# A two-layer hybrid decoder on one core: the indexer moved beside the value projection, and two modulation chunks moved to layer 0

## What is computed

```python
mod = c_act @ ada_w[i] + ada_b[i]                    # 6 x 2048 columns per layer
proj = h @ in_w                                      # q, k, v, qi, wi, ki
qi = apply_rope(qi.reshape(B, L, 16, 64)); ki = apply_rope(ki)      # 16 query heads, one key
wi = wi * 16 ** -0.5
s_idx = einsum('bqhd,bsd->bqhs', qi, ki) * 64 ** -0.5
score = einsum('bqh,bqhs->bqs', wi, relu(s_idx))     # one score for each query and key
score = where(causal, score, -inf)
_, sel = top_k(score, 64)                            # 64 of 256 keys for each query
p = softmax(q @ k[sel].T * 128 ** -0.5)              # 16 heads of 128, only on chosen keys
out = (p @ v[sel]) @ out_w
```

## Time and profile before

| | |
|---|---|
| median of 3 runs | 2574.96 us |
| profiled execution, its own time | 2569.49 us |
| its span, first to last instruction | 2567.7 us |
| TensorE busy | 2434.0 us, 95% |
| VectorE busy | 1811.4 us, 71% |
| ScalarE busy | 1042.8 us, 41% |
| mean granted TensorE clock | 0.974 of 2.4 GHz |
| bytes by DMA | 627.35 MB, mean 244 GB/s |

### The profile page before, as it was taken

One profiled execution on the slowest core, in us unless ns is written; L12 is line 12 of the kernel. 1 busy time (PEld: TensorE's weight loads), 2 busy tenths in 40 slices (PEclk: granted clock), 3 DMA queues, 4 the chain that ended last, 5 costly groups with the idle time before them and its releaser, 6 DMA issues.

```text
span 2567.7 us, 33013 instructions
## 1 busy us (share of the span) xinstructions
PE 2434.0 (95%) x12615; PEld 1942.5 (76%) x12615; DVE 1811.4 (71%) x2796; ACT 1042.8 (41%) x1217; POOL 35.3 (1%) x67
## 2 busy tenths in 40 slices
PE   5898789999999999999999999869999999999998
PEld 2475357878888888888878888748888888888886
DVE  6446988867777767777678877787777755455457
ACT  1353024364443434344453444454644344443442
POOL 0000000000000000000000000000000000000000
PEclk9999899999999999999999999789999999999999
DMA  9856988868888887888658888306588766656664
GB/s 339 325 185 254 375 296 288 280 189 281 300 279 301 293 284 266 279 285 280 196 159 283 278 294 278 126 17 231 170 311 284 251 196 194 188 191 192 193 216 146
DMA packets 310172, 627.35 MB, mean 244 GB/s; under 512 B 30240, under 2 KB 30656, under 8 KB 309760
## 3 DMA queue, kind: packets, MB, share of 16 engines
q1 hardware_dynamic: 305728, 611.35, 70.8%
q0 software_dynamic: 4288, 13.90, 1.8%
HBM read 623.05 MB, written 2.10 MB: 243 GB/s over the span
## 4 chain that ended last, share of the span: by engine, by line
PE 83%; DMA 6%; DVE 5%; issue 2%; ACT 1%; SPq 1%; DVEq 0%; ACTq 0%
PE psB L1842 38%; PE psA L1842 38%; DMA col_raw<-in_ada_w 4%; PE psT L1533 1%; PE psM L1576 1%; PE psM L1563 1%; DVE w_lo L950 1%; DMA w_raw<-in_dsa_in_w 1%; DMA w_raw<-in_s_in_w 1%; PE psT L1722 1%; DMA w_raw<-in_s_glu_w 1%; DVE score L1373 1%; PE psM L1548 0%; ACT w_hi L670 0%; PE psM L1545 0%
## 5 line engine op out<-in xcount | busy, mean ns | idle before, releaser
L950 DVE TENSOR_TENSOR w_lo<-w_raw,w_hi 128x1024 fp32r<-128x1024 f32 x748 | 912.5, 1224 | 619.8 <-ACT w_hi L670 615.9
L670 ACT ACTIVATE w_hi<-w_raw 128x1024 fp32r<-128x1024 f32 x748 | 791.9, 1060 | 1170.0 <-PE psB L1842 479.5
L1842 PE MATMUL psA<-w_hi,hT_hi 128*128 128x512 f32 (+1 forms) x1168 | 457.6, 392 | 9.9 <-issue 3.2
L1842 PE MATMUL psB<-w_hi,hT_hi 128*128 128x512 f32 x1152 | 455.8, 396 | 2.9 <-DVE w_lo L950 2.8
L1842 PE MATMUL psA<-w_hi,hT_lo 128*128 128x512 f32 (+1 forms) x1168 | 454.0, 389 | 0.0
L1842 PE MATMUL psA<-w_lo,hT_hi 128*128 128x512 f32 (+1 forms) x1168 | 453.7, 388 | 0.0
L1842 PE MATMUL psB<-w_hi,hT_lo 128*128 128x512 f32 x1152 | 448.8, 390 | 0.0
L1842 PE MATMUL psB<-w_lo,hT_hi 128*128 128x512 f32 x1152 | 448.5, 389 | 0.0
L967 DVE SCALAR_TENSOR_TENSOR ada_acc<-ada_raw,csil,ada_acc 128x512 f32<-128x512 f32 x420 | 314.0, 748 | 15.3 <-DVE ada_acc L967 0.9
L1842 PEld LDWEIGHTS psA<-w_hi,hT_hi 128*128 128x128 f32 x1168 | 221.5, 190 | 57.1 <-issue 8.7
L1842 PEld LDWEIGHTS psB<-w_hi,hT_hi 128*128 128x128 f32 x1152 | 216.3, 188 | 53.3 <-DVE w_lo L950 6.0
(11 more groups left out here) (344 smaller groups left out, 2107.5 us busy)
## 6 DMA issues: line engine op xcount, KB each, us to landing
w_raw<-in_ffn_w_in SPq DMA_DIRECT2D x352, 512.0 KB, 4.5
ada_raw<-in_ada_w SPq DMA_DIRECT2D x448, 256.0 KB, 5.0
w_raw<-in_ffn_w_out SPq DMA_DIRECT2D x176, 512.0 KB, 4.6
col_raw<-in_ada_w SPq DMA_DIRECT2D x160, 512.0 KB, 6.8
w_raw<-in_dsa_in_w SPq DMA_DIRECT2D x112, 512.0 KB, 4.9
w_raw<-in_s_glu_w SPq DMA_DIRECT2D x64, 512.0 KB, 5.5
w_raw<-in_s_in_w SPq DMA_DIRECT2D x32, 512.0 KB, 3.7
w_raw<-in_dsa_out_w SPq DMA_DIRECT2D x32, 512.0 KB, 5.2
```

The lines of the kernel that those rows point to most:

```text
L670: nc.scalar.activation(high(u), w_raw[:, u % RING], ACT.Copy).then_inc(w_hi_ready, 1)
L950: V.tensor_tensor(low(u), w_raw[:, u % RING], high(u).bitcast(F32), ALU.subtract).then_inc(w_lo_ready, 1)
L1842: ins = MM(PS[s][:, t, 0:r.width], a_[:, kt, tok], b_[:, kk, 0:r.width], start=kt == 0 and m == 0, stop=k == r.units - 1 and kk == UK - 1 ...
```

## The change

**The indexer.** The runs of layer 1 are now `rope`, `idx`, `ki`, `v`, `z`. In `ki` the weights are the stationary operand (80 columns) and the activations of all 256 tokens move, so a unit is six matmuls of 256 columns (`key_products`) in place of twelve of 80; ScalarE and VectorE copy and split only the 80 columns. The result lies transposed in psM and is turned back in `v` (`turn_keys`), roped (`rope_keys`), turned again. The 32 score products, the relus, the weighted sums, the mask, the top-k rounds and `selb` are spread over the 32 units of `v`. The buffers moved out of `hT_hi`, which `v` still reads. `attention()` starts with the logits.

**The chunks.** `v` has no chunks any more. ff1 has five (8 to 12) and ff2 four (15 to 18), with a new spread: the pieces lie evenly over all steps of the run but the last six, 80 in 58 steps and 64 in 42. The numbers of the chunks behind them move by one or two. `ada_acc` has two buffers. In these two runs SP has the pieces of a step ahead of the step's weights.

```diff
-                runs += [Run("rope", 4, dsa_in_w[0], (0, NB), layer=1, ada=[(1, 4, 17)], before="ln"),
-                         Run("v", 2, dsa_in_w[0], (2 * D, 2 * D + NB), layer=1, ada=[(0, 2, 20)]),
+                runs += [Run("rope", 4, dsa_in_w[0], (0, NB), layer=1, ada=[(1, 4, 19)], before="ln"),
                          Run("idx", 1, dsa_in_w[0], (3 * D, 3 * D + NB), layer=1, ada=[(0, 1, 22)]),
                          Run("ki", 1, dsa_in_w[0], (3 * D + IDX_HEADS * IDX_DIM, 0), layer=1),
+                         Run("v", 2, dsa_in_w[0], (2 * D, 2 * D + NB), layer=1),
...
-                ada = [[[(1, 4, 3)], [(0, 4, 8)], [(0, 3, 14)]], [[(1, 4, 24)], [], []]][layer][part]
+                ada = [[[(1, 4, 3)], [], []], [[(1, 4, 24)], [], []]][layer][part]
+                dense = [[None, (8, 5), (15, 4)], [None, None, None]][layer][part]
...
+        def ada_spread(r, i, n):
+            total = r.n * r.per - 6
+            c0, count = r.dense
+            return [divmod(e, AU) for e in range(count * AU) if e * total // (count * AU) == i * r.per + n]
...                                    # SP, in the loop over the steps
+                        if r.dense:
+                            for q_, k in ada_units(r, i, n):
+                                ada_unit(q_, k)
                         if r is glu and i == 0 and n < RING:
                             sp.wait_ge(col_used, glu_after(n))
...
+        def heads_by(step):            # WEIGH_AT = 7
+            first = min(max(3 * (step - WEIGH_AT), 0), IDX_HEADS)
+            second = min(max((5 * (step - WEIGH_AT - 11) + 1) // 2, 0), IDX_HEADS)
+            return first + second
...                                    # VectorE, at each step of v
+            def indexer(step):
+                if step == 2:
+                    rope_keys()
+                if step == WEIGH_AT - 1:
+                    vec.wait_ge(constants, 5)
+                    link(V.tensor_scalar(off[:], causal[:], -MASKED, MASKED, ALU.mult, ALU.add))
+                for n in range(heads_by(step), heads_by(step + 1)):
+                    weigh(n)
+                late = step - WEIGH_AT - 5
+                if late == 0:
+                    hide_later(0)
+                if 1 <= late <= 4:
+                    take_best(0, 2 * late - 2, 2 * late)
+                if late == 5:
+                    select(0)
+                late = step - WEIGH_AT - 17        # tile 1 likewise, rounds in late 1 to 6
...                                    # TensorE, behind each unit of v
+            def scores(step):
+                for n in range(heads_by(step + 1), heads_by(step + 2)):
...
+                    if n >= 4:
+                        pe.wait_ge(idx_relu, n - 3)
+                    MM((T, M)[h // 2 % 2][:, h % 2, 0:N], qiT[rows, h // 2, t * P:(t + 1) * P], kiT[rows, 0:N],
+                       start=True, stop=True).then_inc(idx_full, 1)
+            def key_products(k, u, hi, lo):
+                for kk in range(UK):
+                    kt = k * UK + kk
+                    for m, (a_, b_) in enumerate(((hi, high(u)), (hi, low(u)), (lo, high(u)))):
+                        ins = MM(M[0:key_run.width, 0, 0:SEQ], b_[:, kk, 0:key_run.width], a_[:, kt], ...)
```

More of the change, by code:

```diff
@@ L287, in build, with __init__ @@
         class Run:
-            def __init__(self, kind, n, w, col, row=0, units=KT // UK, layer=0, part=0, ada=(), before=None):
+            def __init__(self, kind, n, w, col, row=0, units=KT // UK, layer=0, part=0, ada=(), dense=None, before=None):
                 self.kind, self.n, self.w, self.row, self.units = kind, n, w, row, units
@@ L320, in build @@
         attn_out = next(r for r in runs if r.before == "attention")
+        key_run = next(r for r in runs if r.kind == "ki")
+        READ_AT, WEIGH_AT = 5, 7
         unit = turn = hs = aT_parts = norms = 0
@@ L1337, in rope @@
                 vec.wait_ge(w_used, product(r, i, s))
-                vec.wait_ge(T_full, r.turn + i * r.turns + (s - 1 if s else -1) if r.kind != "ki" else r.turn)
+                if r is not key_run:
+                    vec.wait_ge(T_full, r.turn + i * r.turns + (s - 1 if s else -1))
                 vec.wait_ge(rope_ready, r.roped + i * r.blocks + s)
@@ new lines, in hide_later, with take_best @@
+            def hide_later(t):
+                N = (t + 1) * P
+                vec.wait_ge(idx_read, (t + 1) * IDX_HEADS)
+                link(V.tensor_tensor(score[:, 1, 0:N], score[:, 0, 0:N], causal[:, t, 0:N], ALU.mult))
+                link(V.tensor_tensor(score[:, 0, 0:N], score[:, 1, 0:N], off[:, t, 0:N], ALU.add))
+            def take_best(t, first, end):
+                N = (t + 1) * P
+                for k in range(first, end):
+                    a, b = k % 2, 1 - k % 2
+                    link(V.max(best[:], score[:, a, 0:N]))
+                    link(V.match_replace(score[:, b, 0:N], best[:], score[:, a, 0:N], TAKEN))
@@ L1907, in _ @@
                         hi, lo = operands(r, i, s, k)
-                        for t in range(TOK):
-                            ins = products(r, s, k, t, u + n, hi, lo)
+                        if r is key_run:
+                            ins = key_products(k, u + n, hi, lo)
+                        else:
+                            for t in range(TOK):
+                                ins = products(r, s, k, t, u + n, hi, lo)
                         ins.then_inc(w_used, 1)
-                        if q is not None and n == r.per - 3:
-                            sum_chunk(q)
+                        for c in ada_ended(r, i, n, 2):
+                            sum_chunk(c)
+                        if r.kind == "v":
+                            scores(i * r.per + n)
                 if splits_last(r):
```

199 lines of the change are left out of this document (113 added, 86 removed).

## The result

Four runs of the changed kernel took 2597.51 to 2600.87 us, median 2598.74; four runs of the kernel before on the same chip 2570.30 to 2575.48, median 2573.56. The ratio is 1.010, 95% interval 1.0083 to 1.0118: 25 us slower, 9 over the forecast of 2590 and inside its own range.

A forecast was written before the change was run, and what follows sets the result against it. TensorE, busy 2434.0 of 2567.7 us, was taken as the bound. The profiled 2569.49 us, minus 33 (indexer), plus 48 (chunks), gave 2584.5; with 5.5 for the median, 2590 us. Own range 2577 to 2612, widened to 2556 to 2622.

The forecast's parts named there:

- the loop through ring, split, copy and landing: ff1 and ff2: weight loads queue on SP behind pieces whose ring slots wait for earlier VectorE splits; price 48 us.
- its turn of L + 3.40: ff1 and ff2: one cycle of held loads takes landing time L plus 3.40 us, 7.4 us at L = 4.0.
- Rival A: ff1 and ff2: loads are not held, the lead swallows all, the whole gain shows; 2542 us, chance 0.08.
- The chunks' part: ff1 and ff2: two more chunks hold weight loads in SP's queue, costing 48 us, bounds 26 and 86.
- ff2*, 30.5 forecast: ff2: a turn spans two units in all of 37 units, 3.70 us a unit against 2.72; 30.5 us lost.
- ff1*, 15.4 forecast: ff1: turns of two and three units alternate, 3.12 us a unit over 53 units; 15.4 us lost.
- rival C: ff1 and ff2: stalls cost more, by 5 us landings or gaps that lower the clock; 2628 us, chance 0.14.
- Rival B: ff1 and ff2: landings shorten to 3.5 us with lighter traffic, price 26 us; 2568 us, chance 0.18.
- The indexer's part: Layer 1: 55.86 us before attention go, 22.6 us come in their place; gain 33 us, between 26 and 39.
- Ki: Layer 1, from idx's end to v's first unit: 12 us, bounds 9 and 16.
- the entry of attention: Layer 1, v's end to the first exp: v's last copy and the exp table load add 1.6 us.
- The scores and the keys' transposes: Inside v of layer 1: score products take 8 us, ends 5 and 13, and key transposes 1 us.

The follow-up runs named there:

- weights first: Changed kernel, but in ff1 and ff2 SP issues a step's weights ahead of its pieces: 2543.76 us, ratio 0.988 to the kernel before.
- ring of 7: Changed kernel, but in ff1 and ff2 SP waits for the piece seven earlier instead of eight: 2695.53 us, ratio 1.048 to the kernel before.
- both orders: Changed kernel, but in ff1 and ff2 SP issues weights ahead of pieces and VectorE uses pieces ahead of the split: 2540.09 us, ratio 0.987.
- the run without the chunks: Kernel before with only the indexer's new run order and new v; v's two chunks left out, ff1 and ff2 as before: 2542.06 us, ratio 0.987.
- ring of 7 and the weights first: Changed kernel, but in ff1 and ff2 SP waits for the piece seven earlier and issues weights ahead of pieces: 2575.66 us, ratio 1.001.

## Why the prediction was right, and where it was off

**The mechanism** held at every link: the loop through ring, split, copy and landing, its turn of L + 3.40, and the two units of ff2. Most of the signs named in advance came: TensorE waits 15.8 us in ff1 and 22.1 in ff2, sums of chunks included (near 15 and 30 forecast), and nowhere in ff0; from unit 5 on the splits of ff2 come every 3.77 us up to unit 42 (3.7 forecast); behind it they come faster than 2.72, since VectorE catches up. Before attention no stretch of layer 1's projections is at 1.2 GHz (1.00 from 1602 to 1715 us). The experiments broke it at the queue, at VectorE and at the ring, and each time the chunks' price fell from 63 us to 2 to 4 us. Rival A (no stall) is out with 2542 us; what it describes is what the order of three lines would have given.

**The chunks' part** was forecast at 48 us and measured 63 (29.1 + 36.2 - 1.9). Against weights first, which has the same work without the stalls, ff1 loses 27.1 and ff2 34.3; the other 2 are TensorE's work for the chunks that came in.

*ff2*, 30.5 forecast, 34.3 measured. The median landing of the units issued in 1105 to 1235 us is 4.0, the value taken:

```profile
DMA to landing us min/median/max: 3.6/4.0/6.5
```

*ff1*, 15.4 forecast, 27.1 measured: 3.37 us a unit from unit 5 to unit 57, where 3.12 were forecast. This is the step that failed. The line of the same 832 to 950 us as in the earlier trace rows:

```profile
DMA to landing us min/median/max: 3.8/5.2/6.5
```

That median mixes two kinds. The table takes the loads one by one from the traces, in the order of SP's queue, from unit 5 on, and sorts them by how many units the order leads back. Under way are the loads and pieces that were issued earlier and had not landed. The last column is the time from the start of the split that releases the load to the start of the load's own split, less the landing.

| run | units back | loads | KB under way at the issue, mean | landing, median us | turn less landing, median us |
|---|---|---|---|---|---|
| after, ff1 | 2 | 15 | 340 | 3.9 | 3.40 |
| after, ff1 | 3 | 38 | 1210 | 5.8 | 3.7, or 4.4 with a second piece |
| after, ff2 | 2 | 37 | 700 | 3.9 | 3.40, or 4.1 with a second piece (4 loads) |
| ring of 7, ff1 | 2 | 53 | 680 | 4.0 | 3.40, or 4.3 with a second piece |
| ring of 7, ff2 | 1 | 21 | 270 | 3.8 | 3.40 |
| ring of 7, ff2 | 2 | 16 | 1020 | 5.4 | 4.4, with a second piece |

So "in a loop that has become the bound there are fewer still. I take 4.0" is right for the units that lead back by two, and wrong for ff1's 38 units that lead back by three: they are issued while more is under way (1210 KB against 340), and land in 5.8 us. Their turn is 9.5 to 10.2 us, 3.2 to 3.4 us a unit, and not the 8.2 us of the forecast, at which such a turn would cost nothing (2.73). For these units the landing is on the side of rival C. "Turns of two units and turns of three alternate" isn't what the order says either: 15 lead back by two and 38 by three. That half costs little: worked through the units with the distances of the order, a lead of 5.8 us and the turn of L + 3.40 (+ 0.8 with a second piece), ff1 loses 13 us at 4.0 throughout, 37 at 5.2 throughout and 31 with the table's two landings; ff2 loses 32 at 4.0. These are estimates, against 27.1 and 34.3 measured. Rival B, with landings of 3.7 us and less, had them moving the other way: the medians of the two-unit turns stayed at 3.9. The Trainium skill's fit of 3.2 us for 512 KB (DMA: Bandwidth & Descriptors, Anatomy of one DMA) is given there for transfers that gpsimd issues, and these are issued by SP, which the prediction left out; by it the time would have been 2558. The medians of these rows, 3.8 to 5.8 us, do not agree with it; one load of both orders, issued at 2328.1 us, took 3.2.

*The clock* was named only in rival C, and belongs in the sum. The record of the granted clock lists six stretches of 3.4 or 6.8 us at 1.2 GHz in ff1 and ff2 of after, 23.9 us in all, and none before. Windows of after, the first such stretch and the time ahead of it:

```profile
868.50:871.90 3.40, 3.40 (x10) 2.63 (x9) 1.42 (x2) 1.06 (x1) 0.00 (x0) 0.50 0.98 343
842.00:868.50 26.50, 23.18 (x103) 18.07 (x102) 16.91 (x19) 9.39 (x9) 0.00 (x0) 1.00 0.77 260
```

In 3.40 us TensorE starts 10 products where at 0.23 us it would be 15. It had stood still for 3.3 of the 26.5 us before. In the earlier trace rows the same place has 12.00 of 12 us busy at 1.00. At half rate 23.9 us lose 12 us of work, part of which would have been spent waiting anyway. Waits (37.9 us listed) and clock (12) leave some 11 of the 61.4 us. An estimate for most of that is the restarts: from 1216.02 to 1218.46 the next start is 2.21 us late where the row lists 2.06 of idleness, and the product behind it starts 0.34 us later where 0.23 is usual. That is 0.26 us, 8 over the 31 waits listed. How much of the clock's loss overlaps with waits is not shown.

**The indexer's part** was forecast at 33 us and measured 32 to 33, by stages and by the run without the chunks. Ki and the entry of attention came within 0.6 us each. The scores and the keys' transposes cost 13.1 us in place of 9. Two score products still start 0.01 us apart at full clock, as at half clock in the earlier trace rows, but two heads of 256 keys cost more than the "half" of 0.43 each: from the last product ahead of them to the second behind them are 1672.87 - 1671.58 = 1.29 us, where two steps of the dense stream are 0.45, so 0.84. Of that, 0.2 us are the turn into the pair and out of it, which comes again at each of v's steps that holds scores. What made up for it is the two chunk sums that left v, which I had set against ff1 and ff2 as "nothing".

**The sum** was off by 31.6 - 15 = 17 us in the span and 9 in the median. That the median came nearer is chance: the 5.5 us put on top of the profiled execution were too many for the changed kernel, whose profiled execution lay 2.1 over its median, and this error of 7.6 us worked against that of the sum. (The last slice of the earlier trace rows is an 8 too, as it is after; nothing in the sum hangs on it.)

## What to carry to other kernels

When a transfer is moved in an in-order queue, follow its wait to the instruction that releases it, and count over how many units of the main stream that release leads back; the stream runs at (landing + the engines' steps) / units, however idle each engine looks. Put the transfers of the stream ahead of those that wait for a background ring, or make the ring longer: either was worth 55 us here. Read the landing for each kind of turn apart, by what is already under way when the load is issued, and add what the granted clock does once a dense stream has recurring gaps.

## What the hardware showed that was not expected

- In a stream that was otherwise dense, recurring waits came with stretches of 3.4 or 6.8 us at 1.2 GHz: 23.9 us of ff1 and ff2 in after (waits of 37.9 us, none over 2.8), 13.6 us with the ring of 7 and the weights first (17.7 us, none over 2.7), 85 us with the ring of 7 (95 us, up to 4.5), and none in before, weights first or both orders, where TensorE never waits.
- The landing of a 512 KB load went with what was under way when it was issued rather than with the mean rate: in after and with the ring of 7 it is 3.8 to 4.0 us with 270 to 700 KB under way, and 5.4 to 5.8 with 1020 to 1210; with the weights first 6.2 with 1600 (37 units of ff1). The mean rate of 832 to 950 us, 277 GB/s before, 257 after and 311 with the weights first, goes with medians of 4.5, 5.2 and 6.1 us. It is a rough relation (before has 4.6 with 1040 KB); what is under way was not varied by itself. With the weights first the longest of these medians cost nothing, since nothing waited in a loop.
- With the weights first DMA moved 285 GB/s over 470 us, and the dense stream never waited. DMA rate bounded neither run.
